# The order of TensorE's three code versions inside the expert loop

## The chip, the cores and the metric

One NeuronCore of a Trainium2 chip runs the whole program. The metric is device time in microseconds (us): the kernel before took 2310.69 us, the median of three runs (2310.22, 2310.69 and 2313.92).

## The reference, cut to what matters

The program is a transformer block with a parallel mixer (sliding-window attention beside an RG-LRU) and a mixture of experts, followed by two layers of a second block, for 256 tokens of width 1024 in float32. Only the experts matter here:

```python
logits = hf @ w_router + b_router                    # 256 tokens, 32 experts
top_vals, top_idx = lax.top_k(logits, 4)             # 4 experts a token
gates = softmax(top_vals)
# each expert, on the tokens that chose it:
gu   = xb @ w_gu[e] + b_gu[e]                        # 1024 -> 2048
gate = minimum(gu[:, :1024], 7); up = clip(gu[:, 1024:], -7, 7)
y    = ((up + 1) * gate * sigmoid(1.702 * gate)) @ w_down[e] + b_down[e]
out  = sum over the 4 experts of gate weight * y
```

The 1024 pairs of token and expert make 32 tokens an expert on average, but the router decides, and the number is known only while the program runs.

## The kernel before, in words

Every engine has a program of its own, written one block after the other. SyncE issues the loads, TensorE (PE) does the products, ScalarE and VectorE do what lies between them. The mixer comes first, then a loop over the 32 experts (`Fori(0, NE)`), then a loop over the two layers.

An expert is worked off in rounds of 64 tokens (`FEW = 64`). There are three versions of its code, written out one after the other in the body of the loop: `expert(e, 4)` with four rounds for more than 128 tokens (`P = 128`), `expert(e, 2)` with two for 65 to 128, `expert(e, 1)` with one for up to 64. At the loop's head PE loads the expert's count into a register (`value_load`, line 1067) and two tests choose the version (lines 1068 and 1071). Each round is, in PE's order: the biases (`bias_hi`, `bias_lo`, line 983), the gate and up products with 8 pieces of weights `gu0` to `gu7` (line 991), the last round's sum into the output accumulators (`combine`, line 968), the transposed choice of tokens (line 1008), the gathering of the next tokens (line 954), transposes of the hidden values (1024) and of the gathered tokens (961), and the down product with the pieces `dn0` to `dn3` (line 1042). ScalarE and VectorE have loops of their own over the experts with the same three versions; the change does not touch them.

The weights of one expert are 12 pieces of 1 MB. SyncE issues them in `load_expert` (lines 612 and 614): the ring in SBUF holds one expert, so a piece of the next expert is issued when PE has used the same piece of this expert in its final round (`gu_used`, `dn_used`). In an expert of several rounds only the final round frees pieces.

Of the kernel before, what the change touches and what calls it, by code (L numbers as in the profile page):

```python
# [22 lines left out]
P = 128  # L23
# [16 lines left out]
FEW = 64  # L40
# [189 lines left out]
def build(nc, dram, out, stop=None):  # L230
# [12 lines left out]
    with ctx:  # L243
# [480 lines left out]
        def _(pe):  # L724
# [340 lines left out]
            pe.wait_ge(bias_ready.sem, 1)  # L1065
            with pe.Fori(0, NE) as e:
                n = pe.value_load(counts_i[0:1, bass.ds(e, 1)], min_val=0, max_val=T)
                with pe.If(n > P):
                    expert(e, 4)
                with pe.Else():  # L1070
                    with pe.If(n > FEW):
                        expert(e, 2)
                    with pe.Else():
                        expert(e, 1)
            pe.wait_ge(y_ready.sem, y_ready.at(R, NE))
            combine().then_inc(combined.sem, R)
            pe.wait_ge(xT_ready.sem, xT_ready.at(R, NE))
# [8 lines left out]
            with pe.Fori(0, NL) as l:  # L1086
# [128 lines left out]
                for i in range(2 * NH + 3):  # L1215
                    if i < 2 * NH:
# [5 lines left out]
                        n = int(name[1])  # L1222
# [20 lines left out]
                    if i >= 4 and i % 2 == 0:  # L1243
                        b = lay(f"o_{att[i - 4]}")
                        for g in (i - 4, i - 3):
                            drained_act(f"t_{att[g]}")
                            n = int(att[g][1])
# [61 lines left out]
        def _(act):  # L1309
# [168 lines left out]
            with act.Fori(0, NL) as l:  # L1478
# [96 lines left out]
                def leading(n):  # L1575

                    name, src, hi, _, free = unit(n)
                    act.wait_ge(*lay_in.here(name, l))
                    act.wait_ge(free[0].sem, free[0].at(free[1], l))
                    f(hi, src, ACT.Copy).then_inc(S["whi"].sem, 1)  # L1580
# [33 lines left out]
        def _(dve):  # L1614
# [311 lines left out]
            with dve.Fori(0, NL) as l:  # L1926
# [142 lines left out]
                def rest(n):  # L2069

                    _, src, hi, lo, _ = unit(n)
                    ready("whi", n + 1)
                    v.tensor_tensor(lo, src, hi.bitcast(F32), ALU.subtract).then_inc(S["wlo"].sem, 1)  # L2073
# [170 lines left out]
```

## Time and profile before

| what | us |
|---|---|
| median of the runs | 2310.69 |
| the profiled execution, its own time | 2322.71 |
| its span | 2320.9 |
| PE busy with products | 2141.1 (92%) |
| VectorE busy | 805.2 (35%) |
| ScalarE busy | 547.8 (24%) |
| the expert loop on PE, first bias product to the last round's end | 188.1 to about 1252 |

Times of rows are microseconds from the span's start. Register, branch and semaphore instructions are not shown as busy time; what the profile calls "issue" is time in which an engine stood idle and waited for no other engine and no transfer that the profile knows of. "q8 instruction" is the queue that brings instructions, in packets. Matmul ends are modelled, and a float32 product stands in the rows as several MATMUL and LDWEIGHTS instructions.

### The profile page before, as it was taken

To read this page: it belongs to the slowest core of one execution; us is meant where nothing else is said; L and a number is where in the kernel's file an instruction comes from. 1 tells how busy PE (TensorE), PEld (TensorE's weight loads), DVE (VectorE), ACT (ScalarE), POOL (GpSimd) and SP (SyncE) were. 2 spreads that over 40 slices of the span, in tenths; PEclk is the share of its full clock that TensorE was granted. 3 is DMA by queue.
4 is the path that set the end of the run, shared out by engine and by line. 5 is a ranking of instruction groups with operands and counts; after the bars stand their busy time and mean duration, and the time that the engine had idled before them with its cause. 6 is when DMAs were issued, how large, how long until landed. Compare 5 with 4: busy or idle time off the path is not lost.

```text
span 2320.9 us, 30840 instructions
## 1 busy us (share of the span) xinstructions
PE 2141.1 (92%) x11550; PEld 1351.6 (58%) x11551; DVE 805.2 (35%) x1442; ACT 547.8 (24%) x902; POOL 25.3 (1%) x45
## 2 busy tenths in 40 slices
PE   6987999988999999999997899998998899998998
PEld 4763333333333333333333787688998787687998
DVE  3531111111221111111222157425863157425873
ACT  1430111111111111111112022404542022404552
POOL 0000000000000000000000020000000020000000
PEclk8997999999999999999998999999999999999999
DMA  9675997089999999999898133234535333234533
GB/s 357 262 319 220 371 418 295 32 357 375 414 418 418 417 418 417 417 418 418 339 418 292 44 122 106 106 110 144 182 101 174 101 122 116 110 109 134 186 109 118
DMA packets 209723, 580.36 MB, mean 250 GB/s; under 512 B 22960, under 2 KB 124592, under 8 KB 173648
## 3 DMA queue, kind: packets, MB, share of 16 engines
q1 hardware_dynamic: 209616, 578.83, 65.1%
q8 instruction: 80, 1.31, 0.3%
q14 instruction: 27, 0.22, 0.0%
HBM read 577.48 MB, written 1.31 MB: 249 GB/s over the span
## 4 chain that ended last, share of the span: by engine, by line
PE 74%; DMA 9%; DVE 7%; SPq 5%; issue 3%; ACT 2%; ACTq 0%; DVEq 0%
PE bank L730 17%; PE bank L991 15%; PE bank L1042 8%; DMA ring<-in_w_gu 8%; PE bank L1285 4%; PE bank L1287 4%; PE bank L1286 4%; SPq L612 3%; PE bank L954 3%; PE bank L968 2%; DVE heap L2020 2%; PE bank L800 2%; PE bank L1301 2%; PE bank L1303 2%; PE bank L1302 2%
## 5 line engine op out<-in xcount | busy, mean ns | idle before, releaser
L991 PE MATMUL bank<-ring,heap 128*64 128x512 f32 x2304 | 519.3, 603 | 18.7 <-DMA ring<-in_w_gu 18.7
L730 PE MATMUL bank<-heap,ring 128*128 128x256 f32 (+2 forms) x1920 | 425.2, 382 | 18.3 <-DVE heap L1965 12.2
L730 PEld LDWEIGHTS bank<-heap,ring 128*128 128x128 f32 (+2 forms) x1920 | 362.0, 189 | 78.2 <-issue 20.4
L991 PEld LDWEIGHTS bank<-ring,heap 128*64 128x64 f32 x2304 | 159.7, 138 | 360.9 <-issue 299.6
L1871 DVE TENSOR_SCALAR heap<-bank 128x256 f32<-128x256 f32 x36 | 15.3, 425 | 770.1 <-PE bank L991 770.1
L1042 PE MATMUL bank<-ring,heap 128*64 128x512 f32 x1152 | 255.1, 595 | 0.0
L1285 PE MATMUL bank<-h_hi,w_hi 128*128 128x256 f32 x704 | 201.2, 286 | 18.2 <-DVE h_lo L2088 18.2
L1286 PE MATMUL bank<-h_lo,w_hi 128*128 128x256 f32 x704 | 200.7, 285 | 0.0
L1287 PE MATMUL bank<-h_hi,w_lo 128*128 128x256 f32 x704 | 200.7, 285 | 0.0
L2073 DVE TENSOR_TENSOR w_lo<-ring,w_hi 128x2048 fp32r<-128x2048 f32 (+1 forms) x68 | 151.6, 2229 | 129.9 <-ACT w_hi L1580 129.9
L1580 ACT ACTIVATE w_hi<-ring 128x2048 fp32r<-128x2048 f32 (+1 forms) x68 | 126.6, 1862 | 179.7 <-PE bank L1287 115.6
L1042 PEld LDWEIGHTS bank<-ring,heap 128*64 128x64 f32 x1152 | 79.6, 137 | 149.9 <-issue 143.9
L1436 ACT ACT_TABLE_LOAD x32 | 41.1, 1283 | 515.4 <-DVE heap L1871 514.9
L1285 PEld LDWEIGHTS bank<-h_hi,w_hi 128*128 128x128 f32 x704 | 136.9, 194 | 19.0 <-DVE h_lo L2088 19.0
L1286 PEld LDWEIGHTS bank<-h_lo,w_hi 128*128 128x128 f32 x704 | 136.9, 194 | 0.0
L1287 PEld LDWEIGHTS bank<-h_hi,w_lo 128*128 128x128 f32 x704 | 136.7, 194 | 0.0
L1301 PE MATMUL bank<-f_hi,w_hi 128*128 128x256 f32 x352 | 101.8, 289 | 8.7 <-DVE w_lo L2073 8.6
L1303 PE MATMUL bank<-f_hi,w_lo 128*128 128x256 f32 x352 | 101.0, 287 | 0.0
L1302 PE MATMUL bank<-f_lo,w_hi 128*128 128x256 f32 x352 | 100.9, 287 | 0.0
L730 PE MATMUL bank<-heap,consts_sb 128*128 128x256 f32 (+1 forms) x180 | 55.5, 475 | 42.8 <-ACT heap L1505 18.6
L2102 DVE SCALAR_TENSOR_TENSOR heap<-bank,vec,heap 128x255 f32<-128x255 f32 x176 | 76.6, 477 | 1.6
L954 PE MATMUL bank<-heap 128*64 128x512 f32 x296 | 73.4, 617 | 3.5 <-DVE heap L1831 3.5
(281 smaller groups left out, 2088.2 us busy)
## 6 DMA issues: line engine op xcount, KB each, us to landing
ring<-in_w_gu SPq DMA_DIRECT2D x256, 1024.0 KB, 16.6
ring<-in_w_down SPq DMA_DIRECT2D x128, 1024.0 KB, 16.3
ring<-in_ffn_w_up SPq DMA_DIRECT2D x44, 1024.0 KB, 7.6
ring<-in_w_ada SPq DMA_DIRECT2D x24, 1024.0 KB, 10.5
ring<-in_w_in SPq DMA_DIRECT2D x24, 1024.0 KB, 7.9
ring<-in_ffn_w_down SPq DMA_DIRECT2D x8, 2816.0 KB, 10.3
ring<-in_w_in SPq DMA_DIRECT2D x7, 2048.0 KB, 10.8
ring<-in_w_out SPq DMA_DIRECT2D x6, 2048.0 KB, 13.6
```

The costliest lines, as they stand in the source:

```text
L730: last = mm(outp, w(k), x(k), start=k == 0, stop=k == nk - 1)
L954: last = mm(psum[2][both[f], :], pick[:, t, FEW * r:FEW * (r + 1)], htok[:, t, 512 * f:512 * (f + 1)], start=t == 0, stop=t == TT - 1)
L991: last = mm(psum[g][both[f], :], xgT[:, k % 4, k // 4, :], wt[:, g, :, f, :], start=False, stop=k == DT - 1, skip_group_check=True)
L1042: last = mm(psum[2][both[f], :], hidT[:, o:o + FEW], wt[:, 512 * f:512 * (f + 1)], start=k == 0, stop=k == DT - 1)
L1285: mm(b[:, g, :], wh, h_hi[:, k, :], start=k == 0, stop=False)
L1286: mm(b[:, g, :], wh, h_lo[:, k, :], start=False, stop=False)
L1287: last = mm(b[:, g, :], wl, h_hi[:, k, :], start=False, stop=k == DT - 1)
L1301: mm(b[:, a, :], wh, f_hi[:, k, :], start=k == 0 and a == 0, stop=False, skip_group_check=True)
L1302: mm(b[:, a, :], wh, f_lo[:, k, :], start=False, stop=False, skip_group_check=True)
L1303: last = mm(b[:, a, :], wl, f_hi[:, k, :], start=False, stop=k == FT - 1, skip_group_check=True)
L1580: f(hi, src, ACT.Copy).then_inc(S["whi"].sem, 1)
L2073: v.tensor_tensor(lo, src, hi.bitcast(F32), ALU.subtract).then_inc(S["wlo"].sem, 1)
```

## The change

In PE's expert loop the two tests are turned round. The test for up to 64 tokens comes first and its version directly behind it, then the test for up to 128 tokens with the version of two rounds, then the version of four rounds. The three bodies are the same as before, every expert runs the same body as before, and the order of the other engines is as it was.

```diff
@@ -1065,13 +1065,13 @@
             pe.wait_ge(bias_ready.sem, 1)
             with pe.Fori(0, NE) as e:
                 n = pe.value_load(counts_i[0:1, bass.ds(e, 1)], min_val=0, max_val=T)
-                with pe.If(n > P):
-                    expert(e, 4)
+                with pe.If(n <= FEW):
+                    expert(e, 1)
                 with pe.Else():
-                    with pe.If(n > FEW):
+                    with pe.If(n <= P):
                         expert(e, 2)
                     with pe.Else():
-                        expert(e, 1)
+                        expert(e, 4)
             pe.wait_ge(y_ready.sem, y_ready.at(R, NE))
```

## Rows read from the trace of the kernel before

**Rows 1.** Page, parts 1 to 3: PE's row; GB/s in 40 slices; instruction queue.

```profile
PE 2141.1 (92%) x11550; PEld 1351.6 (58%) x11551; DVE 805.2 (35%) x1442; ACT 547.8 (24%) x902; POOL 25.3 (1%) x45
GB/s 357 262 319 220 371 418 295 32 357 375 414 418 418 417 418 417 417 418 418 339 418 292 44 122 106 106 110 144 182 101 174 101 122 116 110 109 134 186 109 118
q8 instruction: 80, 1.31, 0.3%
```

**Rows 2.** Waits of PE, 170 to 1252: who waited for what, us, times, longest.

```profile
PE bank L983 <- issue: 32.1, 5, 11.7
PE bank L991 <- DMA ring<-in_w_gu: 18.7, 34, 0.6
```

**Rows 3.** Timeline of PE: first bias product of rounds (start, us, [idle before <-releaser]).

```profile
188.10 0.79 PE L983 MATMUL bank<-bias_hi,bias_sel 64*128 64x512 f32 x1 [2.98 <-issue]
...
230.92 0.78 PE L983 MATMUL bank<-bias_hi,bias_sel 64*128 64x512 f32 x1 [11.67 <-issue]
...
261.08 0.50 PE L983 MATMUL bank<-bias_hi,bias_sel 64*128 64x512 f32 x1
...
371.72 0.49 PE L983 MATMUL bank<-bias_hi,bias_sel 64*128 64x512 f32 x1
...
491.56 0.79 PE L983 MATMUL bank<-bias_hi,bias_sel 64*128 64x512 f32 x1 [9.36 <-issue]
...
525.96 0.49 PE L983 MATMUL bank<-bias_hi,bias_sel 64*128 64x512 f32 x1 [4.78 <-issue]
...
558.57 0.49 PE L983 MATMUL bank<-bias_hi,bias_sel 64*128 64x512 f32 x1 [3.29 <-issue]
...
587.92 0.50 PE L983 MATMUL bank<-bias_hi,bias_sel 64*128 64x512 f32 x1
...
615.59 0.49 PE L983 MATMUL bank<-bias_hi,bias_sel 64*128 64x512 f32 x1
```

**Rows 4.** Busy time by windows: first expert; four rounds (PE (x), PEld (x), ..., PEclk, DMA, GB/s).

```profile
188.10:219.25 31.15, 30.89 (x134) 11.33 (x134) 5.70 (x16) 3.58 (x6) 0.00 (x0) 0.88 0.78 298
371.70:482.20 110.50, 109.69 (x538) 41.49 (x536) 18.13 (x48) 12.97 (x25) 0.00 (x0) 1.00 0.37 151
```

**Rows 5.** DMA queues in windows 175:219, 219:258, 258:371, 371:482, 482:516, 516:600, 600:1252.

```profile
q8 instruction: 5, 0.08, 1.0%
...
q8 instruction: 6, 0.10, 1.5%
...
q1 hardware_dynamic: 8508, 47.02, 101.7%
...
q8 instruction: 5, 0.08, 0.3%
...
q8 instruction: 2, 0.03, 0.4%
...
q8 instruction: 6, 0.10, 0.6%
...
q1 hardware_dynamic: 51249, 266.92, 100.3%
```

**Rows 6.** Timeline of SyncE's queue: issues of gate and up pieces (start, us).

```profile
457.78 12.33 SPq L612 DMA_DIRECT2D ring<-in_w_gu  x8
...
496.71 12.33 SPq L612 DMA_DIRECT2D ring<-in_w_gu  x8
...
530.81 12.33 SPq L612 DMA_DIRECT2D ring<-in_w_gu  x8
...
562.82 13.04 SPq L612 DMA_DIRECT2D ring<-in_w_gu  x8
```

**Rows 7.** Timeline of PE, 1080 to 1180: a round that waits for weights, and the next.

```profile
1083.50 0.49 PE L983 MATMUL bank<-bias_hi,bias_sel 64*128 64x512 f32 x1
...
1099.10 1.94 PE L991 MATMUL bank<-ring,heap 128*64 128x512 f32 x8 [0.56 <-DMA ring<-in_w_gu]
...
1113.62 0.50 PE L983 MATMUL bank<-bias_hi,bias_sel 64*128 64x512 f32 x1
...
1141.29 0.49 PE L983 MATMUL bank<-bias_hi,bias_sel 64*128 64x512 f32 x1
```

## The prediction

> **What bounds the kernel now.** I read the page first, then PE's waits, then the heads of the rounds in PE's timeline, then the queues in windows, then SyncE's timeline. The page shows PE busy for 92% of the span, and in the middle a long stretch in which the transfers run at 417 to 418 GB/s [rows 1]: inside the expert loop two limits change places. PE needs 27.66 us a round: 615.59 - 587.92 = 27.67, and 1141.29 - 1113.62 = 27.67 [rows 3, 7]. An expert's weights need 30.12 us: 12 pieces of 1.049 MB are 12.58 MB, at 417.7 GB/s 30.12 us; the heads 1083.50 and 1113.62 stand 30.12 apart [rows 1, 7]. The loads are the slower, but up to about 780 PE lives on the lead that they have. Once the lead is used up PE waits for gate and up weights, 34 times, 18.7 us in all [rows 2], the last time at 1099.10 [rows 7]. After that a second round, which loads nothing, gives the loads a new lead, and PE alone sets the end.
>
> The other wait is the change's business: 32.1 us of "issue" idleness in five pieces, all directly before the first bias product of a round [rows 2], so at the loop's head: 2.98, 11.67, 9.36, 4.78 and 3.29 us [rows 3]. I call the experts e0 to e31. The pieces stand before e0, e1, and then e7, e8, e9, just behind e6, which is the one expert of four rounds (536 weight loads without a stop = 4 x 134, [rows 4]). The heads of all other experts show no idle time. What distinguishes these five: packets of instructions. They arrive 5 times around e0 and 6 around e1, none in e2 to e5, 5 in e6, 2 and 6 around e7 to e9, and none at all from 600 to 1252 [rows 5]. So TensorE keeps blocks of code, and the stalls are blocks that were thrown out or not yet there.
>
> **How the blocks behave.** 80 packets are 1.31 MB, 16 KB each [rows 1]. In e6 there is about one packet a round (5 in four rounds, [rows 4, 5]), so a round's 134 matmuls and 134 weight loads with what lies around them are slightly more than one block, and the loop with 4 + 2 + 1 rounds lies over about eight: call them 0 to 7, with 8 behind. Before, 0 holds the head, 4 the second test (behind four rounds), 6 the start of the one-round version, 7 its tail and the loop's end. One rule, fitted by me, gives the counts of rows 5: eight places in a ring; a missing block goes into the place behind the one being executed; entering a block fetches its follower if absent; a jump to an absent block stalls.
> - e0 jumps 0 -> 4 -> 6 so early that block 1 is not asked for: packets 4, 5, 6, 7, 8 (five). Coming back to 0, block 1 is fetched over 4, 4 over 5, and so on: 1, 4, 5, 6, 7, 8 (six), two stalls in a row, 11.67 us. Then everything used is there: zero.
> - e6 fetches 2, 3, 4, 5, then stalls for 7 (five); then 8 and 6 (two); then 5, 6, 7, 8, 0, 1 (six). The stalls are those before e7, e8, e9. With seven places the rule gives two packets more in e6, with nine two fewer behind e8's head.
>
> **The change by parts.** After it block 0 holds head and the one-round version up to its last tenth, block 1 its tail and the second test, 1 to 3 the two-round version, 3 to 7 the four-round version, 7 the loop's end. I run the same rule.
> - e0 falls through, no stall at its start: the 2.98 go. At its end it jumps from 1 to 7, which is absent: one stall. Then 0, 1, 2, 7, 8 lie side by side, and e1 to e5 miss nothing.
> - e6 jumps 0 -> 1 (there) -> 3 (absent): one stall at its start. It then fetches 4 to 8 in order and falls into the loop's end: nothing is missing at e7, where block 2 is fetched without anyone waiting. Nothing at e8, e9. The two-round expert (heads 1083.50 and 1113.62) finds 1, 2, 7 and prefetches 3 and 4.
> - Executed tests and jumps: an expert of one round had two taken jumps at its tests, now one not taken and one taken at its end. Nothing else is added; the products that are already in PE's queue hide them, as the heads without idle time show [rows 3]. Nothing of DMA, ScalarE, VectorE or SyncE is moved. I cost these tests and jumps at nothing; uncovered, all of a head's together would cost less than the smallest of the five pieces, 2.98 us, which holds them too [rows 3].
>
> *Price of one stall.* The single one is that before e9: 3.29 us idle (the rest is hidden behind queued products), and e9 itself runs 587.92 - 558.57 = 29.35 instead of 27.66, because the granted clock falls after the idle: 1.69 more. Together 4.98. Bounds: 2.98 (smallest of the five, idle alone) and 11.67 + 2.50 = 14.17 (the pair before e1, whose round takes 261.08 - 230.92 = 30.16). I take 4.98, as both new stalls are single jumps among running loads.
>
> *Start of the loop.* Gone: 2.98 before e0, and before e1 14.17 becomes 4.98. Sum 12.17. e0 itself ran 31.15 us at a granted clock of 0.88 [rows 4], 3.49 over the 27.66; without the idle time before it some of that may go (0 to 3.5). I take 0.
>
> *e6.* Before 371.72 no idle time; now 4.98. So everything up to e6's end is 12.17 - 4.98 = 7.19 us earlier, and the first piece for e7 is issued at 457.78 - 7.19 = 450.59 [rows 6].
>
> *e7 to e9.* PE saves 9.36 + 4.78 + 3.29 = 17.43 of idle time and the slow clock behind it: e7, e8, e9 took 29.62 (to 525.96 less 4.78), 29.32 and 29.35 us, in sum 5.31 over three times 27.66. PE alone would be 7.19 + 22.74 = 29.9 us ahead at e10. But here the loads become the limit. The sets of loads began at 457.78, 496.71, 530.81, 562.82 [rows 6]: 105.04 us for three sets that need 3 x 30.12 = 90.36; the other 14.68 us the queue stood empty, because PE freed nothing. Without the stalls PE frees pieces every 27.66, faster than they are filled, so the loads run without a gap and the fourth set (for e10) starts at 450.59 + 90.36 = 540.95 instead of 562.82. That is 21.9 us earlier. From there on loads run back to back in both kernels until the last wait at 1099.10, so that wait and all behind it (second round, experts to e31, both layers) come 21.9 us earlier. The other 8 us of PE's gain turn into longer waits for `ring<-in_w_gu`: 18.7 us become about 27.
>
> Sum against the profiled execution: 2322.71 - 21.9 = 2300.8. It was taken 12.0 us above the median of the runs; I assume the same difference again, so 2310.7 - 21.9 = **2288.8**.
>
> A rule that speaks against my reading stands in the Trainium skill, "Runtime: NRT & Kernel Launch", section "Instruction fetch mechanics": the instruction memory is only two cache lines, prefetch is purely sequential, and a jump taken outside of these two pages stalls. This case's trace does not agree: 28 of 32 experts show their head without idle time although they jump over four and two rounds, and no packet comes from 600 to 1252. By that rule the jump to the end and the one back would each stall every time, rival C with two stalls a head and some 2,550 us; I give it 1 of the 5% of C.
>
> **Rivals.**
> - A (15%): the new stalls are hidden or do not occur, as block 3 or 7 may be kept. Each is worth 4.98 ahead of e6, and what comes earlier there reaches the end: one gone gives 2283.8, both 2278.8, and a faster clock in e0 up to 3.5 more. For it: 20 us of one round lie between entering the code and the jump. Against: the rule.
> - B (8%): the stalls at the head are not code fetches but the register load and the tests, whose number stays the same: 2310.7. For it: the profile says only "issue". Against: heads without idle time do the same work, and the packets fall just where the stalls are.
> - C (5%), slower: with the end of the loop now four blocks or more behind the one-round version, block 7 is overwritten by the prefetch in every expert, and each jump to the end stalls. Price 4.98 a head, 31 heads: 154 us. PE would be the limit throughout: e0's start at 185.1, 31.15 + 35 x 27.66 + 154.4 makes 1338.8 for the loop's end instead of 1252, so about 2397. It decides from the 12th such stall on: PE's own pace would bring it to the last wait at 587.92 + 17 x 27.66 + 14.0 = 1072.1, so 27.0 us of cover before 1099.1, and with the 29.9 that it gains 56.9, which is 11 stalls. Against: in the old order the same path over three jumps settles after e1.
> - D (10%): the loads between e7 and e10 do not close up, and only what lies ahead of e7 is kept, 7.2 us, or half of the rest: 2303.5 to 2296. For it: the new lead is thin, as e8's first piece is freed at about 477.5 and wanted by the queue at 480.7; a second stall of 3 us there comes through. Against: nothing stalls there by the rule.
>
> **How the numbers follow.** Forecast 62%: 2288.8, on its own 2284 (clock in e0) to 2293 (both stalls paired, 7 instead of 5). With A to D the 80% range is 2280 to 2300. Faster by over 0.2% (4.6 us, about what a measurement of this kernel tells from no change) in the forecast, A and D: 0.87; within 0.2% B, 0.08; slower C, 0.05.
>
> **What would show it.** Right: "issue" idleness before L983 is some 6 to 7 us in two pieces, before e1 and before e6's first round; heads of e0, e7, e8, e9 without any; packets of instructions 3 or 4 in e0 and e1, then none until e6, six to seven there, two in the two-round expert; the waits for gate and up weights grow to about 27 us and begin two or three experts earlier; the last of them near 1077. Wrong: idle time at many heads (C), the five pieces as they were (B), an idle load queue between e7 and e10 (D).

## The result: 2298.5 us against 2318.7 us

The changed kernel took 2298.53 us in the median of 8 runs (2297.44 to 2302.85). The kernel before, run beside it and with the three runs known ahead, took 2318.70 us (2310.22 to 2326.91); ratio 0.992 with a 95% interval of 0.9897 to 0.9943. Faster, as forecast, and 2298.5 lies within 2280 to 2300, but 9.7 us above the 2288.8 that was named. The times of the kernel before fall into two groups, and that will turn out to be the reason. In 24 runs of a later batch 12 lie between 2309.2 and 2316.7 (median 2312.8) and 12 between 2320.8 and 2326.7 (median 2324.4), none between. The changed kernel has one group. It is 14.3 us below the one and 25.9 below the other. (The gap is narrow: among 11 runs of another batch one lay at 2317.3.)

The page of the changed kernel, PE's row, the GB/s of 40 slices and the instruction queue, beside [rows 1]: eleven packets of instructions fewer, and the loads reach 418 GB/s in slice 9 instead of slice 12.

```profile
PE 2135.6 (93%) x11550; PEld 1347.1 (59%) x11551; DVE 805.2 (35%) x1442; ACT 548.0 (24%) x902; POOL 25.4 (1%) x45
GB/s 351 255 341 263 417 417 221 68 418 418 417 418 418 418 419 417 417 418 359 389 418 214 81 99 129 74 147 132 163 128 171 112 117 104 99 112 146 184 102 120
q8 instruction: 69, 1.13, 0.2%
```

PE's waits in the changed kernel (us, times, longest), which answer to [rows 2]: 32.1 us of "issue" idleness at the loop's head became 7.0 in two pieces, and the wait for weights grew from 18.7 to 24.3.

```profile
PE bank L991 <- DMA ring<-in_w_gu: 24.3, 44, 0.6
...
PE bank L983 <- issue: 7.0, 2, 3.7
```

The heads of its rounds, which answer to [rows 3, 7]. The two pieces stand before e1 and before e6's first round (360.33), the places forecast; e7 (472.38) and those behind it have none.

```profile
181.89 0.79 PE L983 MATMUL bank<-bias_hi,bias_sel 64*128 64x512 f32 x1
...
215.44 0.79 PE L983 MATMUL bank<-bias_hi,bias_sel 64*128 64x512 f32 x1 [3.28 <-issue]
...
245.93 0.49 PE L983 MATMUL bank<-bias_hi,bias_sel 64*128 64x512 f32 x1
...
360.33 0.49 PE L983 MATMUL bank<-bias_hi,bias_sel 64*128 64x512 f32 x1 [3.67 <-issue]
...
389.57 0.49 PE L983 MATMUL bank<-bias_hi,bias_sel 64*128 64x512 f32 x1
...
472.38 0.49 PE L983 MATMUL bank<-bias_hi,bias_sel 64*128 64x512 f32 x1
...
555.38 0.49 PE L983 MATMUL bank<-bias_hi,bias_sel 64*128 64x512 f32 x1
...
1059.12 0.49 PE L983 MATMUL bank<-bias_hi,bias_sel 64*128 64x512 f32 x1
...
1074.71 1.94 PE L991 MATMUL bank<-ring,heap 128*64 128x512 f32 x8 [0.56 <-DMA ring<-in_w_gu]
```

Instruction packets of the changed kernel in the windows 178:207 (e0), 207:246 (around e1), 355:471 (e6), 500:1050 (no q8 row, hence none) and 1050:1116 (the expert of two rounds); 471:500 (e7) gives the first row again. The rule fitted ahead gives these counts: block 1; then 2, 7, 8; then 3 to 8; none; then 3 and 4; and block 2 in e7. The profile does not say which block a packet brings, so the counts and the places of the stalls are what agrees; the block numbers are inferred.

```profile
q8 instruction: 1, 0.02, 0.2%
...
q8 instruction: 3, 0.05, 0.5%
...
q8 instruction: 6, 0.10, 0.3%
...
q1 hardware_dynamic: 41138, 229.68, 101.8%
...
q8 instruction: 2, 0.03, 0.2%
```

SyncE's issues of gate and up pieces for e7 to e10, against [rows 6]. The first comes 9.7 us earlier, and then one set follows every 27.6 us, faster than 30.12 us of loading: the load queue never runs dry.

```profile
448.04 12.33 SPq L612 DMA_DIRECT2D ring<-in_w_gu  x8
...
475.65 12.33 SPq L612 DMA_DIRECT2D ring<-in_w_gu  x8
...
503.31 12.32 SPq L612 DMA_DIRECT2D ring<-in_w_gu  x8
...
530.98 12.33 SPq L612 DMA_DIRECT2D ring<-in_w_gu  x8
```

Between the two profiled executions the heads tell where the gain stood: e2 15.15 us earlier (261.08 to 245.93), e10 32.54 (587.92 to 555.38), the expert of two rounds 24.38 (1083.50 to 1059.12), the end 24.74 (2322.71 to 2297.97). So 8.2 us of PE's 32.5 went into the limit of the loads. Only 5.6 of them stand in the list of waits. A round that the loads limit takes 30.12 us instead of 27.67, but its listed waits are three of about 0.56 us; the rest of the 2.45 us stands inside the product rows. By the heads, the stretch of 17 experts from e10 to the expert of two rounds took 495.6 us before and 503.7 now, where 17 free rounds of 27.67 would take 470.4.

Set against b_pad64 below, an execution of the old order without the stall before e1, the changed kernel is 3.84 us ahead at e2, 22.26 at e10, 14.15 at the expert of two rounds and 13.36 at the end. There, too, 8.1 us are given back, and the end is close to the 14.3 us to the lower group.

### The profile page after: what moved, and what is told of

Same layout as the page of the kernel before. It is cut to its first block, busy times and chain, and to the rows that moved or that the text cites. A ratio compares the mean times of both kernels' runs of the same rounds, so it can differ in the third digit from the quotient of the medians.

```text
span 2296.2 us, 30840 instructions
## 1 busy us (share of the span) xinstructions
PE 2135.6 (93%) x11550; PEld 1347.1 (59%) x11551; DVE 805.2 (35%) x1442; ACT 548.0 (24%) x902; POOL 25.4 (1%) x45
## 3 DMA queue, kind: packets, MB, share of 16 engines
HBM read 577.48 MB, written 1.31 MB: 252 GB/s over the span
## 4 chain that ended last, share of the span: by engine, by line
PE 71%; DMA 11%; DVE 7%; SPq 6%; issue 3%; ACT 2%; ACTq 0%; DVEq 0%
PE bank L730 17%; PE bank L991 14%; DMA ring<-in_w_gu 9%; PE bank L1042 8%; SPq L612 4%; PE bank L1285 3%; PE bank L1287 3%; PE bank L1286 3%; PE bank L954 2%; PE bank L968 2%; DVE heap L2020 2%; PE bank L800 2%; PE bank L1301 2%; PE bank L1302 2%; PE bank L1303 2%
## 5 line engine op out<-in xcount | busy, mean ns | idle before, releaser
L991 PE MATMUL bank<-ring,heap 128*64 128x512 f32 x2304 | 518.9, 601 | 24.3 <-DMA ring<-in_w_gu 24.3
L730 PE MATMUL bank<-heap,consts_sb 128*128 128x256 f32 (+1 forms) x180 | 55.8, 478 | 43.2 <-ACT heap L1505 18.7
L1450 ACT ACTIVATE heap<-bank 128x512 f32<-128x512 f32 x36 | 21.5, 597 | 231.5 <-PE bank L1042 231.5
```

The lines of the kernel that those rows point to most:

```text
L730: last = mm(outp, w(k), x(k), start=k == 0, stop=k == nk - 1)
L991: last = mm(psum[g][both[f], :], xgT[:, k % 4, k // 4, :], wt[:, g, :, f, :], start=False, stop=k == DT - 1, skip_group_check=True)
```

## The experiments

**The kernel before again.** Unchanged: 10 runs, and once more in a later batch.

> The kernel before, unchanged, a second time. Its times so far fall into two groups, about 2311 and about 2325 us. Block theory: they differ in whether block 1 of the loop was fetched before e0's first jump; if this profile is of the fast group, the idle time before e1 (11.67 us before) is gone and only 2 to 3 packets of instructions instead of 6 come around e1; if it is of the slow group, it looks as the first profile did. Rival (the groups come from the transfers or the clock): fast and slow profiles both show the 11.67 us before e1, and the 13 us lie elsewhere.

> The kernel before once more, for a profile of its fast group. If it is of the fast group: 6 packets of instructions around e0, none around e1, no idle time before e1, and the head of e10 about 12 us earlier than 587.9. If it is of the slow group: as before.

10 runs of the first split 5 and 5 (2309.1 to 2316.4, 2323.4 to 2327.5); the profile (2325.5 us of span) and that of the third (2323.7) both fell into the upper group: 11.24 and 11.14 us idle before e1. b_third differs from the first in one thing, the start of e0: its products of line 1062 ran at a faster clock, 4.34 us instead of 7.19, and yet e0's head stands where it stood, at 188.26 against 188.10, with 6.02 us of idle time before it instead of 2.98.

```profile
177.91 4.34 PE L1062 MATMUL bank<-heap 32*128 32x256 f32 x16
188.26 0.78 PE L983 MATMUL bank<-bias_hi,bias_sel 64*128 64x512 f32 x1 [6.02 <-issue]
```

So e0's head waited for code, and the products ahead of it only hid part of that wait. In 175:219 b_third has six packets and in 219:258 five, the first profile five and six: eleven in both. All three profiles of this kernel at full load are of the upper group. That the lower group lacks just this stall was not seen at full load on the unchanged kernel.

**64 more instructions ahead of the loop.** The head lies deeper in its block, and PE passes the block's start earlier.

```diff
             drained_mix("ht3")
+            for _ in range(128):
+                pe.wait_ge(vec1_in.sem, 32)      # long since true; two waits an instruction
             pe.wait_ge(pick_ready.sem, 1)
```

> The kernel before with 64 more instructions on PE (128 waits on a semaphore that has long come) well ahead of the loop, where PE waits for VectorE anyway, so that the loop's head lies 64 instructions deeper in its block and the follower is asked for before e0 jumps. Block theory: no idle time before e1, 14 us less than the slow group, always about 2311 us; the three stalls at e7, e8 and e9 stay (9.4, 4.8, 3.3). Rival: both groups and the idle time before e1 stay as they are.

2311.60 us in 12 runs, 2308.1 to 2315.8, all in one group; ratio to before 0.9974 (0.9956 to 0.9992). Heads of e0 and e1, then the packets of 175:222 and the q1 row of 222:250, which has no q8 row beside it:

```profile
191.17 0.79 PE L983 MATMUL bank<-bias_hi,bias_sel 64*128 64x512 f32 x1 [6.46 <-issue]
...
222.09 0.50 PE L983 MATMUL bank<-bias_hi,bias_sel 64*128 64x512 f32 x1
```

```profile
q8 instruction: 6, 0.10, 1.1%
...
q1 hardware_dynamic: 1995, 11.57, 101.0%
```

The 11.67 us before e1 are gone, six packets come around e0 (by the rule block 1 is now among them) and none around e1. The upper group is gone with them. The idle time before e0 is 6.46 us. The extra waits stand in the rows as 6.0 us of issue idleness before the gathering, where 3.5 us of waiting for VectorE stood, but no price is seen in the time: 2311.60 is 1.2 us below the lower group's median. Why is open.

> The changed kernel with the same 64 instructions ahead of the loop. Block theory: the head falls through into block 1 and is not sensitive to it: two stalls of 3.3 to 3.7 us, 2298.5 us within 2. Rival (PE's position in the code decides by itself, or the waits cost time): more than 3 us off.

2300.94 us (2300.2 to 2303.5), 0.9935 (0.9911 to 0.9959), 2.4 us above the changed kernel, a little outside the 2 that I gave. There are two stalls, 2.13 before e1 (said: 3.3 to 3.7) and 3.57 before e6, and again one group. I take the 2.4 us as the price of the waits; as b_pad64 shows none, that is not shown. With the 64 instructions in both, neither kernel has the stall of 11 us before e1, and the change gives 2311.60 - 2300.94 = 10.7 us. That is the fairest measure of the order alone.

**Lighter loads.** Only the first half of each down-product piece is loaded, in both kernels; the other half of the product reads stale data.

```diff
-    sp.dma_start(piece(exp_stream, name, 2), dn[:, 2 * j:2 * j + 2, :]).then_inc(...)
+    sp.dma_start(piece(exp_stream, name, 2)[:, 0:1, :], dn[:, 2 * j:2 * j + 1, :]).then_inc(...)
```

> The kernel before with the second half of each down-product piece left out of the load (the product reads what lies in the ring there), 8 MB + 2 MB instead of 12 MB an expert, so about 25.1 us of loads against 27.66 us of PE: the loads are no limit any more. Two-limits theory: no waits for in_w_gu in the loop; the stalls at the head stay (a little shorter, as the queues are emptier); about 2306 us in the slow group, 2292 in the fast one. Its partner a_light should be 28 to 33 us below the slow group or 16 to 19 below the fast one, more than the 25.7 and 13.5 that the change gives with the full loads. Rival (the change's gain is all there is, the loads hide nothing): the difference stays at 25.7 and 13.5.

> The changed kernel with the same lighter loads. Two-limits theory: about 2274 us (2298.5 less the 24.3 us of waits for in_w_gu), two stalls at heads; the rest as for b_light.

2281.65 us (four runs at 2279.7 to 2282.1, two at 2289.7 and 2292.0) against 2265.29 (2260.5 to 2269.0). The waits for `in_w_gu` are gone from both. Both levels came out lower than I said, by 9 to 15 us. I had read the price of the loads off the list of waits (18.7 and 24.3 us). The rounds give more: for the 18 from e10 to the last that the loads limit, 495.6 + 30.1 less 18 x 27.67 = 27.6 us before and 35.8 in the changed kernel, of which the medians show 31.7 (with the shorter stalls, 7.99, 3.31 and 2.37 behind e6) and 33.2. The differences of the medians, about 16 and 25.5 us, are no larger than with full loads, so the times do not decide between the theories. The heads do. First the kernel before, e0, e1, e10 and e31, then the changed one, e10 and e31:

```profile
188.12 0.79 PE L983 MATMUL bank<-bias_hi,bias_sel 64*128 64x512 f32 x1 [6.80 <-issue]
...
218.16 0.50 PE L983 MATMUL bank<-bias_hi,bias_sel 64*128 64x512 f32 x1
...
572.07 0.50 PE L983 MATMUL bank<-bias_hi,bias_sel 64*128 64x512 f32 x1
...
1180.75 0.49 PE L983 MATMUL bank<-bias_hi,bias_sel 64*128 64x512 f32 x1
```

```profile
554.38 0.49 PE L983 MATMUL bank<-bias_hi,bias_sel 64*128 64x512 f32 x1
...
1163.04 0.49 PE L983 MATMUL bank<-bias_hi,bias_sel 64*128 64x512 f32 x1
```

17.69 us ahead at e10 and 17.71 at e31: with light loads nothing is given back, where with full loads 8.2 of 32.5 were. And this profile is the nearest to the one that was missing: it lies in the lower group of its kernel, PE's program is that of the kernel before to the instruction, and here e1 has no idle time. e0 has more, 6.80 us. Packets in 175:219, and the window 219:350 has none:

```profile
q8 instruction: 6, 0.10, 1.3%
...
q1 hardware_dynamic: 8085, 49.59, 96.0%
```

Six around e0, and none around e1 instead of six. Two of them come in 178.5:179.5, where the three upper profiles have none before 180 and one in 180:181. So the same PE program does the one or the other. That it depends on whether the follower is asked for before the jump, a race, is my reading; the profile shows the packets, not the requests.

**How many blocks are kept.** An island of 700 instructions that nobody executes, and two of them, ahead of the one-round version.

```diff
                 with pe.If(n <= FEW):
+                    for _ in range(2):              # one island: range(1)
+                        with pe.If(n > P):
+                            for _ in range(1400):
+                                pe.wait_ge(vec1_in.sem, 32)
                     expert(e, 1)
```

> The changed kernel with an island of 700 instructions that nobody executes, jumped over ahead of the one-round version. The path of an expert of one round then touches seven different blocks, followers among them (0, 1, 2, 3, 4 and the loop's end with its follower). Ring-of-eight theory: no packet of instructions and no stall in e2 to e5 and from e8 to e26, single stalls at e1, e6, e7, e27 and e28: 2303 to 2318 us. Rival C (the distant end of the loop is lost in every expert): stalls at all heads, above 2400 us.

> The same with two such islands: the path now touches nine different blocks, one more than eight. Ring-of-eight theory: nine packets and four stalls in each of the 30 experts of one round, one behind the other at the head, 15 to 22 us idle before each first bias product and about 45 to 50 us an expert: 2,800 to 3,000 us. Rival (other number of places, or a replacement by age that keeps the head): few or no stalls, within 30 us of the run with one island.

One island: 2342.9 us (2341.0 and 2344.9), 25 above the range; two islands: 2925.5 us (2923.7 and 2927.4). With one island there is no stall and no packet from 650 to 1080, as said. What I missed: 12.1 us before e1 and 3.65 before e2, which look like the lost race again, and waits as long as pairs of stalls where I had said single ones, 9.35 us before e7 and 14.18 behind the expert of two rounds. There the rule, as I applied it, failed. With two islands nine blocks are touched, and every head stalls. Two heads and the packets between them (1004:1054), then the sum of waits:

```profile
1004.83 0.79 PE L983 MATMUL bank<-bias_hi,bias_sel 64*128 64x512 f32 x1 [19.95 <-issue]
...
1054.30 0.79 PE L983 MATMUL bank<-bias_hi,bias_sel 64*128 64x512 f32 x1 [18.78 <-issue]
```

```profile
q8 instruction: 9, 0.15, 1.7%
```

```profile
PE bank L983 <- issue: 582.5, 32, 21.2
```

Nine packets an expert and 49.5 us, as the ring of eight says. Seven blocks keep, nine do not; a path of exactly eight was not tried. This is the state that rival C describes, produced by 1400 instructions more in the loop.

**Other orders.** First the outer test `n > FEW` with two and four rounds behind it and one round last, here with 64 instructions ahead of the loop (diffs shortened).

```diff
+                with pe.If(n > FEW):
+                    with pe.If(n <= P): expert(e, 2)
+                    with pe.Else():     expert(e, 4)
+                with pe.Else():
+                    expert(e, 1)
```

> Third order: the outer test is n > FEW, behind it the versions of two and four rounds, and the version of one round last, directly ahead of the loop's end, so that an expert of one round jumps once forward and falls into the end; 64 instructions ahead of the loop as before. Block theory: e0's jump to block 6 stalls under the products that are queued ahead of the loop, so nothing or under 1 us is seen; e1 to e5 none; one stall before e6; none after it. About 5 us less than the changed kernel: 2293.5 us. Rival (the order of the change, one round directly behind the head, is what counts): 2298 or more, as before's order.

2299.85 us (2297.0 to 2301.7), 0.9924 (0.9897 to 0.9951), 6.4 above the 2293.5 that I had said, in the range of the rival, and 1.1 below a_pad64. Not one visible stall but three: 1.02 before e0, and these before e6 and e7:

```profile
357.67 0.49 PE L983 MATMUL bank<-bias_hi,bias_sel 64*128 64x512 f32 x1 [3.09 <-issue]
...
474.48 0.62 PE L983 MATMUL bank<-bias_hi,bias_sel 64*128 64x512 f32 x1 [4.68 <-issue]
```

The one before e7 follows if a follower that is found present moves the ring's pointer (the place that is filled next) on too, once there was time to look. I tested that with the same order and fewer instructions ahead, placed in front of `drained_mix("ht3")`:

> The third order again (outer test n > FEW, two and four rounds, one round last), with 32 instead of 64 instructions ahead and put where PE is idle anyway. Rule as corrected by the first run of this order (a follower that was found moves the pointer on): e0 stalls under queued products, two single stalls before e6 and e7, none before e1. The 2.4 us that the 64 instructions cost are gone: 2297 to 2298 us, the same as the changed kernel within 0.2%. Rival (32 instructions are too few, block 1 is not asked for in time): 11 us idle or a single stall before e1 and 2302 to 2310 us.

2296.95 us (2296.6 to 2298.8), 0.9901 (0.9866 to 0.9935), as said, but by another way: 1.88 us before e0, 3.23 before e6 and none before e7. So the corrected rule fails here and the first holds. When the pointer moves on stays open; it looks like a second race. This is the fastest kernel of the study, 1.6 us below the changed one, which is within 0.2% and no difference that these runs prove. What both runs of this order do show is that the one-round version need not stand directly behind the head: placed last, it is as fast.

The order one, four, two:

```diff
                 with pe.If(n <= FEW):
                     expert(e, 1)
                 with pe.Else():
-                    with pe.If(n <= P): expert(e, 2)
-                    with pe.Else():     expert(e, 4)
+                    with pe.If(n > P):  expert(e, 4)
+                    with pe.Else():     expert(e, 2)
```

> Order one round, four rounds, two rounds. Ring-of-eight theory: the four-round version now starts in block 1, so no stall at e6's start, but its end jumps from block 5 to 7 and then back to 0, both absent: two stalls in a row before e7, 9 to 12 us idle; before e1 3.3 as in the changed kernel. Two-limits theory: e7's loads start 5 us earlier than in the changed kernel (about 443 instead of 448), and of the 11 us before e7 some 6 are lost for the load queue, so the time is within 2 us of the changed kernel: 2298 to 2301. If the loads hid nothing (every us of PE counts) it would be 2304 to 2305.

2304.74 us (2301.7 to 2309.0), 0.9931 (0.9909 to 0.9952): the packets and stalls came as forecast (3.21 before e1, none before e6, a pair before e7), the time did not: it is 6.2 above the changed kernel and lies in the 2304 to 2305 of the rival by which the loads hide nothing. Head of e7 and the issues for e7 and e8:

```profile
476.13 0.78 PE L983 MATMUL bank<-bias_hi,bias_sel 64*128 64x512 f32 x1 [10.44 <-issue]
```

```profile
441.28 12.33 SPq L612 DMA_DIRECT2D ring<-in_w_gu  x8
...
482.00 12.93 SPq L612 DMA_DIRECT2D ring<-in_w_gu  x8
```

From 441.28 to 482.00 are 40.7 us for 30.1 us of loads: 10.6 lost, not 6, against 6.8 won by the earlier start. That makes 3.8 more than the changed kernel; its later heads are 4.5 behind (1063.63 against 1059.12), while PE at e8 is 6.96 behind (507.01 against 500.05). So the loads hid 2.4 of the 6.96 us, less than I had subtracted. The median alone does not speak against the rival; the heads do.

## Why the prediction was right and where it failed

*Two limits, five stalls, one ring of blocks:* right for the changed kernel. The packets came in the windows where the rule put them. Both new stalls had the size of single ones (3.28 and 3.67 us, taken as 3.29). With the slow clock behind it, e6's cost 3.67 + 29.24 - 27.60 = 5.31 instead of 4.98, and e1's 3.28 + 30.49 - 27.67 = 6.10. One reading was miscounted: five stalled heads leave 27 of the 32 experts without idle time, not 28. The argument for which it was used, that most heads do not stall, stands. That the count of blocks is eight is bounded by the islands (seven, nine), and they also show a layout in which the rule foresaw too little.

*Start of the loop:* mis-sized, 15.15 us instead of 12.17. e0's head came 6.21 us earlier, where the sum had 2.98. Before e1 the idle time went as forecast, 11.67 - 3.28 = 8.39; e0 itself ran 0.88 faster and e1 0.33 slower. In the term before e0 I took the idle time for the whole price of the wait, but part of the wait lay under the 16 products of line 1062. They took 7.19 us before and 4.41 in the changed kernel, whose clock was 0.87 of full speed in 176:180 where before it was 0.50. Before, then after, windows 176:180 and the rows of line 1062:

```profile
176.00:180.00 4.00, 3.70 (x13) 0.50 0.01 2
```

```profile
176.00:180.00 4.00, 3.70 (x19) 0.87 0.01 4
```

```profile
177.93 7.19 PE L1062 MATMUL bank<-heap 32*128 32x256 f32 x16
...
177.56 4.41 PE L1062 MATMUL bank<-heap 32*128 32x256 f32 x16
```

These products stand ahead of everything that was changed, and the unchanged kernel can run them fast too (4.34 us in b_third), so I take the clock as chance of the execution. What it brings is not: in the old order b_third's faster products bought nothing, e0's head stayed at 188.26 behind 6.02 us of idle time, while in the new order nothing is waited for there and the head follows the products.

*e7 to e9:* right in the mechanism and near in size. Three quarters of PE's gain come through: 32.54 ahead at e10, 24.38 at the expert of two rounds; the difference, 8.16, was forecast as 8. The listed waits for weights rose to 24.3 instead of about 27, since the list holds only part of what the loads cost; the last stands at 1074.7 instead of near 1077. For the profiled execution the sum said 2300.8, and 2297.97 was measured, 2.8 less, about what the start of the loop gave beyond the forecast (2.98).

*"I assume the same difference again":* this step failed. The 12.0 us between the profiled execution and the three runs were not a constant of profiling: the changed kernel's profiled execution, 2297.97, lies 0.6 us below the median of its runs. They are the distance of the two groups, and what the runs show in the place of the assumption is the stall before e1. The profiled execution had it, the three runs (2310 to 2314) lay in the lower group, and the prediction took its removal, 11.67 + 2.50 less 4.98, off times that did not contain it. From the lower group the change gives 14.3 us, from the upper 25.9, and 21.9 could hold for neither. The profile held the clue: I had noted that e0 jumps "so early that block 1 is not asked for", and had 12.0 us unexplained beside a stall of that size. b_pad64 shows that the upper group goes when the stall goes, b_light that the same PE program can run without it. A profile of the unchanged kernel's lower group at full load is still missing, so for those three runs this is inferred.

*Luck:* 2298.5 lies within the stated range, but not for the reasons that made its width (the clock in e0, paired stalls, the rivals): the group of the three runs was not among them. It also lies in the span of rival D, 2296 to 2303.5, whose mechanism the issues every 27.6 us exclude.

*Rivals:* A, B and D did not occur. C did not in the changed kernel, but two islands produce its state.

## What to carry to other kernels

Where a loop has several large bodies on TensorE, look at the instruction queue's packets in windows: stalls called "issue" at a loop's head that coincide with packets are code that was not there. Keep the 16 KB blocks that the common path touches, followers included, few: here seven cost nothing and nine stalled every time. And look at where a long, rare body ends: ahead of the loop's end or of the common body its fetches left one stall or none behind it, ahead of the two-round version (o142) a pair. Whether the common body stands first or last made no difference that these runs prove. Before a sum is subtracted from a median, ask whether the profiled execution belongs to the same group as the runs: a difference of a stall's size between the two is a term, not an offset.

## What the runs showed of the hardware

- TensorE keeps blocks of 16 KB of code (80 packets, 1.31 MB). A path that by the inferred layout touches seven fetched nothing from 650 to 1080; one that touches nine fetched nine packets an expert, idled 18 to 21 us at nearly every head and took 49.5 us instead of 27.7. The limit lies between; eight fits the counts. The Trainium skill, "Advanced Engine Details and Errata", section "ISA Cache", gives 128 KB and lines of 16 KB for TensorE, which agrees, and "Only 2 cache lines!", which these runs contradict.
- With full loads, a jump to an absent block left, from e1 on, 2.1 to 3.7 us of idle time where the rule has a single one, 4.1 to 4.8 in some places (before e8 in the old order, before e7 in s24_pad64), and what the rule has as a pair 9.3 to 14.2 us. Part of the wait lies under queued products: with these at 7.19 or at 4.34 us, e0's head stood at 188.10 and 188.26, behind 2.98 and 6.02 us.
- After such idle time the granted clock was at its lower level, 1.2 GHz (0.50 in 215.44:219 of the changed kernel), and the round behind it took 1.6 to 3.4 us longer.
- One PE program can fetch in two ways. 24 runs of one kernel lie in two groups 11.6 us apart; the three profiles of the upper group have 11.1 to 11.7 us idle and five or six packets at e1, and b_light, with the same PE program and lighter loads, neither.
